# Identity products into unread PSUM columns at TensorE's known waits in a two-layer diffusion backbone

## The reference, cut to what matters

```python
for i in range(DEPTH):                       # DEPTH = 2
    h_lat = rmsnorm(x_lat, norm_w[i, 0]) * (1 + sc_l) + sh_l
    h_ctx = rmsnorm(x_ctx, norm_w[i, 0]) * (1 + sc_c) + sh_c
    y_lat, y_ctx = mixer_i(h_lat, h_ctx)     # hgrn2, then mamba2
    x_lat = x_lat + g_l * y_lat
    x_lat = x_lat + g2_l * swiglu(rmsnorm(x_lat, norm_w[i, 1]) * (1 + sc2_l) + sh2_l,
                                  ffn_w_in[i], ffn_w_out[i])
    ...                                      # the context likewise in layer 0
return rmsnorm(x_lat, final_norm_w)
```

## Time and profile before

| | us |
|---|---|
| median of 3 runs | 2121.7 |
| lowest, highest | 2121.1, 2123.09 |
| profiled execution, its own time | 2116.36 |
| its span, first to last instruction | 2114.6 |
| PE busy | 2039.2 |
| DVE busy | 1275.2 |
| ACT busy | 863.0 |
| mean granted TensorE clock | 0.989 |

### The profile page before, as it was taken

The page is one execution under the profiler, slowest core; times in us unless marked ns, Lnnn a source line. Parts: engine busy times, 40 slices in busy tenths (PEclk is TensorE's granted clock), DMA queues, the critical chain, the costliest instruction groups (busy, mean ns, idle before and its releaser), DMA issues.

```text
span 2114.6 us, 33441 instructions
## 1 busy us (share of the span) xinstructions
PE 2039.2 (96%) x12674; PEld 1802.4 (85%) x12674; DVE 1275.2 (60%) x1958; ACT 863.0 (41%) x1392; POOL 114.3 (5%) x175
## 2 busy tenths in 40 slices
PE   6999999999999999999999999999998999999998
PEld 4899999998889999999998877778775787888887
DVE  7655655557475773764766767777777644333335
ACT  4544433434232341332433555748384325222222
POOL 1111001010010000000000100000000000000000
PEclk9999999999999999999999999999999999999999
DMA  8422232323422432433322221221216223333332
GB/s 311 140 81 83 68 90 81 91 61 120 119 87 78 138 116 80 138 96 96 98 88 66 77 70 41 66 64 50 89 48 230 64 86 86 93 99 97 93 99 90
DMA packets 297916, 204.68 MB, mean 97 GB/s; under 512 B 5396, under 2 KB 289421, under 8 KB 296013
## 3 DMA queue, kind: packets, MB, share of 16 engines
q1 hardware_dynamic: 294349, 180.04, 29.0%
q0 software_dynamic: 3456, 23.09, 3.0%
HBM read 189.47 MB, written 13.63 MB: 96 GB/s over the span
## 4 chain that ended last, share of the span: by engine, by line
PE 81%; DVE 8%; ACT 5%; issue 3%; DMA 1%; SPq 1%; ACTq 0%; POOL 0%; DVEq 0%; POOLq 0%
PE G L328 56%; PE G L1241 13%; ACT e L1995 1%; PE S L2133 1%; PE S L874 1%; DVE acc L2164 1%; PE S L2129 1%; PE S L845 1%; PE S L453 1%; DVE wlo L315 1%; DVE hlo L755 1%; DVE hn L746 1%; ACT whi L311 1%; PE G L437 1%; DMA ada<-in_ada_w_dram 1%
## 5 line engine op out<-in xcount | busy, mean ns | idle before, releaser
L328 PE MATMUL G<-hhi,whi 128*128 128x384 f32 (+2 forms) x1760 | 573.9, 377 | 25.5 <-DVE hlo L755 16.2
L315 DVE TENSOR_TENSOR wlo<-raw,whi 128x1024 fp32r<-128x1024 f32 (+2 forms) x213 | 248.0, 1165 | 471.9 <-ACT whi L311 471.3
L328 PE MATMUL G<-hhi,wlo 128*128 128x384 f32 (+2 forms) x1760 | 531.4, 352 | 0.0
L328 PE MATMUL G<-hlo,whi 128*128 128x384 f32 (+2 forms) x1760 | 531.0, 352 | 0.0
L311 ACT ACTIVATE whi<-raw 128x1024 fp32r<-128x1024 f32 (+2 forms) x213 | 215.9, 1014 | 718.6 <-PE G L328 584.5
L328 PEld LDWEIGHTS G<-hhi,whi 128*128 128x128 f32 x1760 | 318.8, 190 | 92.0 <-issue 39.6
L328 PEld LDWEIGHTS G<-hhi,wlo 128*128 128x128 f32 x1760 | 326.5, 190 | 20.1
L328 PEld LDWEIGHTS G<-hlo,whi 128*128 128x128 f32 x1760 | 327.1, 190 | 17.7
L328 PE MATMUL G<-mhi,whi 128*128 128x384 f32 (+2 forms) x544 | 163.6, 349 | 2.0 <-issue 0.9
L328 PE MATMUL G<-mhi,wlo 128*128 128x384 f32 (+2 forms) x544 | 162.6, 347 | 0.0
L328 PE MATMUL G<-mlo,whi 128*128 128x384 f32 (+2 forms) x544 | 162.5, 347 | 0.0
(11 more groups left out here) (356 smaller groups left out, 2991.6 us busy)
## 6 DMA issues: line engine op xcount, KB each, us to landing
raw<-in_ffn_w_in_dram SPq DMA_DIRECT2D x52, 512.0 KB, 4.0
raw<-in_ssm_w_in_dram SPq DMA_DIRECT2D x41, 512.0 KB, 4.0
raw<-in_hg_w_in_dram SPq DMA_DIRECT2D x40, 512.0 KB, 4.1
adaw<-in_ada_w_dram SPq DMA_DIRECT2D x20, 1024.0 KB, 5.3
adaf<-in_ada_w_dram SPq DMA_DIRECT2D x20, 1024.0 KB, 5.3
sraw<-in_ffn_w_in_dram SPq DMA_DIRECT2D x36, 512.0 KB, 5.1
raw<-in_ffn_w_out_dram SPq DMA_DIRECT2D x32, 384.0 KB, 3.6
raw<-in_ssm_w_out_dram SPq DMA_DIRECT2D x16, 512.0 KB, 4.1
```

Source lines behind the costliest of these rows:

```text
L315: dve.tensor_tensor(wlo[pn.slot][:, 0:kt, :], raw[pn.slot][:, 0:kt, :], f32(whi[pn.slot][:, 0:kt, :]), ALU.subtract).then_inc(s["lo"], 1)
L328: ins = pe.matmul(G[:, tl.slot, g0:g0 + n], w[pn.slot][:, k, :], r[:, k_base + k, t0:t0 + n], start=(first and k == 0 and i == 0), stop=(l ...
```

## The change

A helper `keep_busy(pe, to, n)` issues n plain products of the 128 x 128 identity with itself (4-byte floats) into columns of PSUM that nobody reads. They wait for nothing of their own and signal nothing; each stands ahead of a wait that PE already had. There are 7 before norm 0's first block, 7 and 5 before slabs 0 and 1, 11 in norm 1 (6 in e = 0, of which 4 before block 3, and 5 in e = 1), 13 in norm 2 (7, of which 4 before block 4, and 6), 8 in norm 3 (5, of which 4 before block 2, and 3), 5 before `dt_turn`, and 2 and 5 in the last group: 63 in all. Nothing is removed or moved.

```diff
--- before.py
+++ after.py
@@ -384,6 +384,16 @@
 
         SUMS_AT, SPREAD_AT, TURN_FIRST = 4, 10, 6
 
+        def keep_busy(pe, to, n):
+
+            for _ in range(n):
+                pe.matmul(to, ident[:, :], ident[:, :], start=True, stop=True)
+
+        def unread(slot, bank=1):
+            return G[:, slot, (bank + 1) * BANK - P:(bank + 1) * BANK]
+
+        BESIDE = {1: ((0, 1, 1, 4, 0), (1, 1, 1, 1, 1)), 2: ((0, 1, 1, 1, 4), (2, 2, 2)), 3: ((0, 1, 4), (1, 1, 1))}
+
         def product_pair(pe, N, pn, tl, segs, rows=None):
 
 
@@ -396,6 +406,8 @@
                     if e == 0 and k == STREAM[N] + 4:
                         spread_half(pe, N, 1, segs)
                     if k < KT:
+                        if k < len(BESIDE[N][e]):
+                            keep_busy(pe, unread(tl.slot, 0 if e and len(segs) == 2 else 1), BESIDE[N][e][k])
                         pe.wait_ge(s["hlo"], 16 * N + 8 * e + k + 1)
                         ins = product_block(pe, pn, tl, m["hhi"], m["hlo"], k, KT, segs, half=e, apart=False)
                     if k == KT - 1:
@@ -1784,6 +1796,8 @@
             for u in range(2 * KT + LAG[0]):
                 if u < 2 * KT:
                     e, k = norm_place(0, u)
+                    if u == 0:
+                        keep_busy(pe, unread(pn.slot), 7)
                     pe.wait_ge(s["hlo"], u + 1)
                     ins = product_block(pe, pn, pn, m["hhi"], m["hlo"], k, KT, SEGS, half=e, apart=False)
                 if u == 2 * KT - 1:
@@ -1952,6 +1966,7 @@
             product_pair(pe, N2, At(PAN_DT), At(PAN_DT), SEGS)
 
         def dt_turn(pe):
+            keep_busy(pe, unread((PAN_SS + DT_TURN[0]) % 2), 5)
             pe.wait_ge(s["dtd"], 1)
             H2 = 2 * NH
             for i, src in enumerate(("cumS", "dln", "dzt")):
@@ -2259,6 +2274,8 @@
                         heads_y(pe, q, hh - 1)
                 if (j, k) == (7, 3):
                     heads_y(pe, q, HPG - 1)
+                    if ss is None:
+                        keep_busy(pe, S[:, 0, 0:P], 2)
                 if (j, k) == (7, 5):
                     pe.wait_ge(s["ym2"], HPG * q + HPG)
                     for i_ in range(GT):
@@ -2271,6 +2288,8 @@
                         ins = pe.matmul(group_sums(ss)[:, b:b + 1], block(m["wx0"][:, :], b), ones[:, :],
                                         start=True, stop=True)
                     ins.then_inc(s["ysum"], 1)
+                if (j, k) == (8, 4) and ss is None:
+                    keep_busy(pe, S[:, 3, 0:P], 5)
                 if (j, k) == ((8, 4) if ss is None else SPREAD_BESIDE):
                     spread_pe(pe, q + RSTD_GROUPS, range(LBLK), group_factors(ss))
                 if ss is not None and (j, k) == (9, KT - 1):
@@ -2803,6 +2822,7 @@
             pe.wait_ge(s["csil"], 1)
             pe.wait_ge(s["ps"], N_PICK)
             for i in (0, 1):
+                keep_busy(pe, S[:, 3, BANK - P:BANK], (7, 5)[i])
                 slab_strips(pe, i)
             for i in (0, 1):
                 pe.wait_ge(s["modev"], i + 1)
```

## The result

The changed kernel took 2110.09 us (median of 7 runs, 2106.16 to 2115.74) against 2121.85 (7 runs, 2120.16 to 2125.55). The ratio is 0.995, interval 0.9937 to 0.9962, so 10.6 us less, between 8.1 and 13.4 (the medians are 11.8 apart). The direction was forecast rightly.

A forecast was written before the change was run, and what follows sets the result against it. PE, busy for 96% of the span, was taken as the bound, by its work and what it waits for. 1.2 + 2.7 + 0.5 + 1.4 + 0.5 - 0.1 = 6.2 us off 2121.7 gave 2115.5 us, range 2110.5 to 2120.5.

The forecast's parts named there:

- norm 1: Sums and 12 products at full clock give 2.6 us; the fall mostly stays, so 1.2 counted.
- norm 2: 24 products and the sums give 4.4 us at most, 3.4 taken because DVE limits; 2.7 counted.
- norm 3: DVE's wait for the spread is all that can go, 1.1 us; 0.5 counted.
- last group: 0.3 us if the clock holds, most lost in a wait; 0.5 counted as other runs may fall at later waits.
- The price of an identity product: Each added product costs 0.135 us at full clock, 0.25 at half; all 63 cost 8.5 or 15.8 us, mostly inside waits.
- Does it hold?: Shares by PE's busy time ahead of each fall: norm 1 to 2.57 us of 4.70, norm 2 to 4.08 of 5.00.
- step sizes: Small products and ACT's copies ahead of the turn give 2.2 us; not every run falls there, so 1.4 counted.
- The first: Rival: the clock holds at every place, 9.6 us won, 2112.1 us; chance 0.10.
- The second: Rival: every half-clock microsecond in all eight stretches counts half, 21.8 us won, 2099.9 us; chance 0.03.
- The third: Rival: added products too little or misplaced, clock still falls at most places; gain 0 to 4.2 us, 2119.7 us; chance 0.22.
- the fourth: Rival: added products displace work at half clock at norms 1 and 2; 5 us slower, 2126.7 us; chance 0.08.
- a sum of 0: By the skill page only long idle gaps lower the clock in mid-kernel; no norm wait is one, so nothing is won.

The follow-up runs named there:

- e3: Changed kernel with every added product moving one column instead of 128; 2124.51 us against 2122.38 for the kernel before, ratio 1.001.
- e5: Changed kernel with one transpose in place of each of the 63 products; 2113.68 us against 2122.14 for the kernel before, ratio 0.9961.
- e8: Changed kernel without the 19 start products, four added before the last group's sums, four in layer 0's feed-forward network; 2108.13 us, ratio 0.9931 to the kernel before.
- e9: The changed kernel once more, unchanged; 2111.49 us against 2121.62 for the kernel before, ratio 0.9954.
- e10: Changed kernel without its 19 products at the start; 2111.96 us, ratio 0.9953 to the kernel before.
- e6: Changed kernel with only the five products ahead of the step sizes' turn kept; 2119.09 us against 2122.14 for the kernel before, ratio 0.998.
- e7: Changed kernel with only the last group's 2 + 5 products kept; 2117.9 us, ratio 0.9977 to the kernel before.
- e11: Changed kernel with only norm 1's 11 products kept; 2117.99 us against 2121.62 for the kernel before, ratio 0.9984.
- e12: Changed kernel with only norm 2's 13 products kept; 2116.9 us, ratio 0.9978 to the kernel before.
- e4: Changed kernel with two transposes in place of each added product; 2111.43 us, ratio 0.9951 to the kernel before.

## Why the prediction was right or wrong

**What bounds it.** Right. The won time is products that ran at half clock behind waits; e3 shows it, since the same instructions without their columns win nothing.

**The price of an identity product.** Wrong by half. The prediction counted loads in the earlier trace rows as products. Each is two instructions, 0.27 us. The cover was mostly there for twice the price: at norm 1 PE still waits up to 1.0 us for `hlo` in the profile after, where it was 1.87. In the last group it was not there when the clock was down: 2.33 us of added work made the spread 1.2 us late. That cost stood in the text for norm 2's block 4 and came at another place.

**Does it hold?** These shares made the forecast too low. The comparison of stretches was made with half of the work that is added: norm 1's was to go to 2.57 us of 4.70, and is 3.04. At norm 2 it counted all seven products ahead of the fall, but only three stand in that stretch; the four ahead of block 4 come behind its end. It came to 4.08 of 5.00, with two errors that nearly cancel, and is 3.80. Nor would the right figure have told: 3.04 of 4.70 is about as full as 3.13 of 5.00, at which the clock fell before, and it held in five profiles of seven. So the price is shown to be wrong, and that it explains the shares is argued. Taking the mean over the profiles with the full products in place less the mean over those without any (e3 and e5 left out, in the last group e8 too), by the table:

```
              forecast   all held, forecast   profiles
norm 1          1.2            2.6               2.2
norm 2          2.7            3.4               3.0
step sizes      1.4            2.2               0.9
last group      0.5            0.3               0.3
norm 3          0.5            1.1               1.5
start           0              0                 0.0
```

The values by chain were good: 2.3, 3.6, 2.2 and 1.2 us in the first row of the profile table, for 2.6, 3.4, 2.2 and 1.1. The share at norms 1 and 3 was too low. At the step sizes it was too high, as the clock does not fall there in every execution of a kernel without them; the prediction had named that. The sum of the last column is 7.9 us, from which the late end takes 1.75; the runs say 10.6 (8.1 to 13.4) and 9.8 (7.0 to 12.5) in e9.

**The end.** The prediction put it at nothing, as no DMA is added. Two packets more of code are loaded, and the output lands 1.75 us later behind DVE's last result. This term was missing.

**The start.** No gain of its 19 products is seen: the profiles' means are alike, and e10 equals e9. With the end's 1.75 us, which e10 does not have, and an interval of some 2.7 us either way, a gain of 1 to 2 us is not excluded.

**From the profile to the median.** The 5.3 us between them was taken as a constant. It was luck of one execution. Six of the seven executions after lie within 4.3 us of the median on either side, the profiled one 2.6 above it, where that of before lay 5.3 below. So the pair of profiles shows 3.7 us, less than the 6.2 forecast from one to the other, and only the medians show 10.6.

**The rivals.** The first (all held, 2112.1) is nearest to the measured time, and in the profile after it holds at four of six places. The second, half of all half-clock time, is out: it asked for 21.8. Over many executions it fares no better. The mean clock of the 20 executions of before beside e9 is 0.9853, of the seven after 0.9964; the differences from 1 are twice that in time at half clock, so 62 and 15 us, 47 us less, for 10 to 12 us won. A microsecond at half clock cost 0.21 to 0.26 us here, not the 0.5 of the Trainium skill's page "TensorE: Matmul & The Clock Gate", section "Terms". The likely reason, argued and not tried by itself, is that PE waits for DVE or a DMA in much of that time at either clock. The third and the fourth did not come. The rule that the prediction cites for a sum of 0, that of long idle gaps, is contradicted by each profile without the products.

**What stays open.** The places' 7.9 us less the end's 1.75 are 6.2, and the runs give 10.6: some 4 us are in no stretch of these profiles, and one profile of each kernel (two of the changed one) can't say where. The singles e6, e7, e11 and e12 give 4.2, 4.9, 3.4 and 4.7 us, 17.2 together without norm 3, where the whole kernel gives 10.6; the late end, which no single has, is 1.75 of the gap. Each interval is about 2 us to either side, but all four lie above what their own stretch shows in the profiles (0.9, 0.3, 2.2, 3.0). Whether that is chance, or whether an added wait-filler also shifts where later falls come, no run tells. Nor is it settled how often norm 1 holds: five of seven profiles with its products do.

## What to carry to other kernels

A wait of TensorE costs a second time if the clock falls behind it, and products into columns that nobody reads buy that back as long as they end before the wait does: here 10.6 us for 126 instructions. Look at the granted clock stretch by stretch in more than one execution, since where it falls moves, and fill only waits behind which PE's work is on the chain; the 19 products at the start bought nothing that the runs can show. Look at the end too: more instructions move the loads of code, and here one came into the output. Size the filler for half clock too, where it takes twice as long and can hold up what it stands in front of.

## What the runs showed of the hardware

- A plain product of 4-byte floats is two matrix instructions and two loads; a transpose, and a product of the rounded 4-byte type, is one.
- Weight loads do not keep the clock up: with 126 of them and one column each it fell at norms 1 to 3 and the step sizes as before (e3), at norm 2 for 10.1 us with the load unit busy for all of it.
- Transposes keep it up as plain products do (e4, 10.4 us). The Trainium skill, page "TensorE: Matmul & The Clock Gate", section "Part 4: PE-mode transpose", says that they don't count as busy in the same way; these runs don't agree.
- A 16 KB load of code in the midst of the output transfers goes with their landing late: a median of 4.2 to 4.6 us from issue to landing where it was 3.1 without, 1.07 to 1.85 us more at the end in four profiles of four, nothing in the ten without it.
- The same kernel's executions differ by up to 10 us (2106.16 to 2115.74) on one core, and the granted clock goes with it: 0.999 in the fastest, 0.994 in the slowest.
